# Two transformer blocks on one core: the first feed-forward's down product as seven block products

## The reference

```python
h2 = rms_norm(x, norm2_g[l])
up = h2 @ w_up[l]                      # 1024 x 5632: gate and value
up = causal_depthwise_conv(up, ffn_dw_w[l])   # width 3, along the tokens
gate, val = jnp.split(up, 2, axis=-1)
x = x + (jax.nn.silu(gate) * val) @ w_down[l]  # 2816 -> 1024
```

## Time and profile before

| | |
|---|---|
| median of 3 runs | 2779.06 us |
| profiled execution | 2782.16 us, of which span 2780.5 us |
| granted TensorE clock, mean | 0.992 of 2.4 GHz |
| TensorE busy | 2714.4 us (98%) |
| VectorE, ScalarE, GpSimd busy | 1758.4, 1131.0, 640.6 us |
| DMA | 414 MB, mean 149 GB/s |

### The profile page before, as it was taken

The page is one execution under the profiler, slowest core; times in us unless marked ns, Lnnn a source line. Parts: engine busy times, 40 slices in busy tenths (PEclk is TensorE's granted clock), DMA queues, the critical chain, the costliest instruction groups (busy, mean ns, idle before and its releaser), DMA issues.

```text
span 2780.5 us, 31459 instructions
## 1 busy us (share of the span) xinstructions
PE 2714.4 (98%) x12219; PEld 2197.0 (79%) x12219; DVE 1758.4 (63%) x2235; ACT 1131.0 (41%) x1590; POOL 640.6 (23%) x548
## 2 busy tenths in 40 slices
PE   9989999999999999999999999999999999999997
PEld 7877668788888788888878888766777888888886
DVE  6886554689999843243324444566548787776567
ACT  4423442343433443221235655665345322223543
POOL 1213111000110042010002222113423244444113
PEclk9999999999999999999999999999999999999999
DMA  3224532334444464344623232666543365657874
GB/s 123 84 83 140 145 80 103 140 104 122 130 121 121 157 234 138 117 150 157 214 84 102 69 99 85 173 183 189 195 169 125 137 213 188 204 189 248 262 251 133
DMA packets 147283, 414.45 MB, mean 149 GB/s; under 512 B 18616, under 2 KB 23352, under 8 KB 147136
## 3 DMA queue, kind: packets, MB, share of 16 engines
q1 hardware_dynamic: 115024, 309.97, 34.3%
q0 software_dynamic: 32112, 102.48, 11.9%
HBM read 309.46 MB, written 102.92 MB: 148 GB/s over the span
## 4 chain that ended last, share of the span: by engine, by line
PE 79%; DVE 12%; ACT 4%; issue 3%; DMA 2%; POOL 1%; SPq 0%; DVEq 0%; POOLq 0%; ACTq 0%
PE ps L218 77%; DVE cacc L189 3%; PE ps L221 2%; ACT PB L183 1%; POOL ga L186 1%; DVE cv L189 1%; DVE PB L189 1%; DVE tr L189 1%; DVE tl L186 0%; DVE YA L186 0%; DMA raw<-in_w_win 0%; DVE sqacc L186 0%; DVE ps L198 0%; DVE T L189 0%; DMA RBc<-scr_inv 0%
## 5 line engine op out<-in xcount | busy, mean ns | idle before, releaser
L218 PE MATMUL ps<-AH,wh 128*128 128x512 f32 (+1 forms) x1104 | 446.0, 404 | 19.4 <-DVE T L186 7.0
L218 PE MATMUL ps<-AH,wl 128*128 128x512 f32 (+1 forms) x1104 | 432.0, 391 | 0.0
L218 PE MATMUL ps<-AL,wh 128*128 128x512 f32 (+1 forms) x1104 | 431.6, 391 | 0.0
L218 PEld LDWEIGHTS ps<-AH,wh 128*128 128x128 f32 (+1 forms) x1104 | 206.6, 187 | 72.2 <-issue 10.4
L218 PE MATMUL ps<-stk,stk 128*128 128x512 f32 (+3 forms) x832 | 245.1, 409 | 12.8 <-DVE small L198 6.9
L218 PEld LDWEIGHTS ps<-AH,wl 128*128 128x128 f32 (+1 forms) x1104 | 206.5, 187 | 46.6
L218 PEld LDWEIGHTS ps<-AL,wh 128*128 128x128 f32 (+1 forms) x1104 | 207.0, 187 | 44.4 <-issue 2.9
L218 PEld LDWEIGHTS ps<-stk,stk 128*128 128x128 f32 x832 | 147.9, 191 | 83.2 <-issue 34.0
L186 DVE TENSOR_TENSOR wl<-raw,wh 128x1024 fp32r<-128x1024 f32 (+1 forms) x76 | 112.7, 1484 | 150.2 <-ACT wh L183 135.0
L218 PE MATMUL ps<-euh,ewt 128*128 128x512 f32 x640 | 198.8, 391 | 2.1 <-DVE eul L186 2.1
L186 POOL TENSOR_TENSOR wl<-raw,wh 128x1024 fp32r<-128x1024 f32 (+3 forms) x47 | 102.0, 2171 | 319.3 <-ACT wh L183 319.2
(11 more groups left out here) (324 smaller groups left out, 6373.6 us busy)
## 6 DMA issues: line engine op xcount, KB each, us to landing
ewr<-in_dn SPq DMA_DIRECT2D x88, 256.0 KB, 3.2
pwr<-in_w_up SPq DMA_DIRECT2D x38, 512.0 KB, 4.1
swr<-in_w_gu SPq DMA_DIRECT2D x38, 512.0 KB, 4.1
raw<-in_w_w2in SPq DMA_DIRECT2D x32, 512.0 KB, 4.2
scr_u<-cv SPq DMA_DIRECT2D x22, 512.0 KB, 2.6
eur<-scr_u SPq DMA_DIRECT2D x44, 256.0 KB, 3.4
scr_u<-uu SPq DMA_DIRECT2D x22, 512.0 KB, 8.6
alr<-in_dn POOLq DMA_DIRECT2D x11, 1024.0 KB, 9.9
```

The lines of the kernel that those rows point to most:

```text
L218: return Issued(self, self.e.matmul(out, l, r, start=start, stop=stop, skip_group_check=onto))
```

## The change

FF1's down product uses seven block products with 11 steps each (77 steps, `DOWN1`, `INTO1`), with four sums of weight blocks (`s_s1`) and four of activation blocks (`s_t1`), both kept in DRAM.

1. `weight_sums` in `pool_a`: 88 transfers from DRAM to DRAM of 256 KB in 8 phases of 11 (44 copies, 44 that add), four behind each low part of tiles 4 to 25. From phase 2 on, a phase waits until all before have landed.
2. `block_sums` in `pool_ff1`: GpSimd loads a pair of spilled stages, makes four sums, stores them; 11 times, nine within the up part.
3. Down part: both streams are loaded and split at each step (77 + 77), all low parts on VectorE; passes accumulate onto banks of earlier passes and are evacuated in between.
4. Up part: the seven products go to three banks (bank 0: X11, T2, T3, T4; bank 1: T1, X22; bank 2: X21), double-buffered over pairs; X22 and T3 change places. ScalarE copies bank 0 after X11 and after T2 and bank 1 after T1; `shared` and `shared_end` on VectorE go. `value` (one half) stands before the low parts of the next pair's second group, `gate_end` and `value_scaled` behind, `value_end` is one scaled evacuation.
5. `sums_high` first negates two of the four sums on ScalarE.
6. Value weights are loaded in three transfers with waits of their own, the first two earlier. The first two stage tiles of the down part have other homes (free later), and the last three weight rows use slots 6 to 8.
7. The next stage works in banks 4 to 7 at first, its norm sums in other banks.

```diff
+            for x in range(4 * (s - 4), min(4 * (s - 3), 8 * NK)):   # pool_a, behind w_low(s)
+                if x >= 0:
+                    weight_sums(x)
...
+        def weight_sums(x):
+            phase, k = divmod(x, NK)
+            a11, a21, a12, a22 = [self.io["dn1"][2 * k + i, h, :, :] for i in range(2) for h in range(2)]
+            s2, s3, s4, s1 = [self.io["s_s1"][i, k, :, :] for i in range(4)]
+            if phase > 1:
+                q.wait_ge(S.jd1, 16 * phase * NK)
+            if phase == 0:
+                q.dma(s1, a21).then_inc(S.jd1, 16)
+            elif phase == 1:
+                q.dma(s3, a11).then_inc(S.jd1, 16)
+            elif phase == 2:
+                q.dma_add(s1, a22, max_dma_last_dim=8192).then_inc(S.jd1, 16)
+            elif phase == 3:
+                q.dma_add(s3, a21, max_dma_last_dim=8192).then_inc(S.jd1, 16)
...
+            odd = self.TR1[k][:, 1:4:2, :]          # sums_high
+            q.act(odd, odd, ACT.Copy, scale=-1.0).then_inc(S.th1)
+            q.wait_own()
             q.act(self.TH1[k], self.TR1[k], ACT.Copy).then_inc(S.th1)
...
             for i in range(7):                      # pe_ff1, up part
+                if i == 0:
+                    q.wait_ge(S.uev, 2 * (PLAIN + n - 1) if n else 0)
+                elif i == 2:
+                    q.wait_ge(S.snp1, 3 * n + 1)
+                elif i == 4:
+                    q.wait_ge(S.snp1, 3 * n + 2)
+                elif i == 5:
+                    q.wait_ge(S.snp1, 3 * n + 3)
+                elif i == 6:
+                    q.wait_ge(S.ev1, 3 * n + 2)
                 part(n, i)
-        for w in range(88):
+        for w in range(7 * NK):
...
             taken(n)                                # act_ff1, per pair
             if n:
                 silu(i)
             if n + 1 < NQ:
+                high(n + 1, 0)
+            taken_shared(n)
+            if n + 1 < NQ:
+                high(n + 1, 4)
+            else:
+                d_high(0)
+                u_high(0)
+            taken_fifth(n)
+            if n + 1 < NQ:
+                high(n + 1, 5)
+                high(n + 1, 2)
...
             if n:                                   # dve_ff1, per pair
                 value_end(n - 1)
                 taps(0, i)
+                taps(1, i)
             gate(n)
             if n:
                 gated(i)
             if more:
                 s_sums(n + 1)
+                s_lows(n + 1, 0)
             value(n)
             if more:
+                s_lows(n + 1, 2)
+            gate_end(n)
+            value_scaled(n)
+            if more:
+                s_lows(n + 1, 1, 3)
...
+        def block_sums(j):                          # pool_ff1
+            q.wait_ge(S.tl1, 4)
+            q.wait_ge(S.jd1, self.SUMS1_END + 16 * j)
+            q.wait_ge(S.du1, 32 * j + 32)
+            for x in range(2):
+                q.dma(self.TW1[:, 2 * x:2 * x + 2, :], self.io["s_u1"][2 * j + x, :, :]...).then_inc(S.jl1, 16)
+            ...four q.tt(..., ALU.subtract), each waiting for the one before
+            q.dma(self.io["s_t1"][j, :, :, :], self.TW1[:, :, :]).then_inc(S.jd1, 16)
```

More of the change, by code:

```diff
@@ L381, in __init__ @@
         self.EU, self.EUR, self.EU_FREE = [], [], []
[L382 to L389, removed]
+        homes = [("g", k, 0, 1) for k in range(4)] + [("g", 4, 0, 2), ("g", 5, 0, 2), ("g", 4, 1, 6), ("g", 5, 1, 6)]
+        homes += [("a", k, 1, 7) for k in (0, 1, 2)] + [("a", 6, 1, 7), ("a", 7, 1, 7)]
+        homes += [("a", k, 1, 7) for k in (4, 5, 3)] + [("g", k, 1, 7) for k in range(4)]
         for which, k, half, free in homes:
@@ L395, in __init__ @@
             self.EU_FREE.append(free)
+        for x in range(2):
+            one = Area(nc, sq + 4096 * x, sq + 4096 * x + 4096)
+            self.EUR.append(Area(nc, one.lo + 2048, one.hi).get("eur", [P, 512])[:, :])
+            self.EU.append(tuple(one.get("eu", [P, 512], F32R)[:, :] for _ in range(2)))
+            self.EU_FREE.append(7)
+        self.TW1 = Area(nc, sq, sq + 8192).get("tw1", [P, 4, 512])
         w = Area(nc, lo + 4096, TOP)
@@ L1558, with f1_bank @@
     PAIRS1 = [(part, i) for i in range(PLAIN) for part in ("g", "v")]
-    SHAPE1 = [("X11", 0), ("X21", 1), ("T2", 5), ("T1", 4), ("X22", 6), ("T3", 2), ("T4", 3)]
-    E_FREE = {slot: max(w for w in range(88) if w % DW == slot) for slot in range(DW)}
+    SHAPE1 = [("X11", 0), ("X21", 1), ("T2", 5), ("T1", 4), ("T3", 2), ("X22", 6), ("T4", 3)]
+    def f1_bank(self, n, x):
+        return self.bank(4 * ((n + 1) % 2) + x)
+    DOWN1 = [(("a", 0, 0), ("b", 0, 1)), (("a", 1, 0), ("b", 1, 1)), (("s", 0), ("t", 2)), (("s", 3), ("t", 1)),
+             (("s", 1), ("t", 0)), (("s", 2), ("b", 1, 0)), (("a", 1, 1), ("t", 3))]
+    INTO1 = [((0, 1, ALU.subtract),), ((0, 1, ALU.subtract),), ((0, 0, ALU.subtract),),
+             ((0, 0, ALU.add), (4, 0, ALU.subtract)), ((4, 0, ALU.add),), ((0, 0, ALU.subtract),), ((4, 1, ALU.add),)]
+    SUMS1_END = 16 * 8 * NK
+    SQUARES1 = [(1, n) for n in range(4)] + [(0, n) for n in (4, 5, 6, 7, 0, 1, 2, 3)] + [(1, n) for n in range(4, 8)]
+    E_SLOT = [w % DW for w in range(74)] + [6, 7, 8]
+    E_FREE = {slot: max(w for w in range(77) if w < 74 and w % DW == slot or w == 68 + slot > 73) for slot in range(DW)}
     def f1_tile(self, x):
@@ L1620, in part @@
             name, b = self.SHAPE1[i]
-            out = self.s_bank(n, i)
-            q.wait_ge(S.sl1, 4 * n + {0: 1, 1: 1, 5: 2, 6: 2, 4: 3, 2: 4, 3: 4}[b])
+            out = self.f1_bank(n, (0, 2, 0, 1, 0, 1, 0)[i])
+            first, onto = i in (0, 1, 3), i not in (0, 1, 3)
+            q.wait_ge(S.sl1, 4 * n + {0: 1, 1: 1, 4: 2, 5: 3, 6: 3, 2: 4, 3: 4}[b])
             h, l = self.p_high(n, b), self.p_low(n, b)
@@ L1628, in part @@
                 xh, xl = self.sums1(name, k)
-                q.mm(out, h[:, ws], xh, k == 0, False)
-                q.mm(out, h[:, ws], xl, False, False)
-                t = q.mm(out, l[:, ws], xh, False, k == 3)
+                q.mm(out, h[:, ws], xh, first and k == 0, False, onto)
+                q.mm(out, h[:, ws], xl, False, False, onto)
+                t = q.mm(out, l[:, ws], xh, False, k == 3, onto)
             t.then_inc(S.prd1)
@@ L1742, in act_ff1 @@
         tap_value(1)
-        for b in (0, 5, 4, 2):
+        for b in (0, 4, 5, 2):
             high(0, b)
@@ L1804, in act_ff1 @@
+                q.act(self.sqF[m % 2][:, :], self.XR[:, n, c], ACT.Square).then_inc(self.squared1(m)[0])
+        for w in range(6, 7 * NK):
+            d_high(w)
+            u_high(w)
+            if 52 <= w < 56:
+                square(w - 52)
+            if 63 <= w < 67:
+                square(4 + w - 63)
+                into(0, 4 + w - 63)
+            if 72 <= w < 76:
+                square(8 + w - 72)
+                into(0, w - 72)
         for n in range(4):
@@ L2159, in sp_ff1 @@
         u_load(9)
-        for w in range(9, 88):
+        for w in range(9, 7 * NK):
             d_load(w)
-            if w < 21:
+            if w < 7 * NK - 1:
                 u_load(w + 1)
```

363 lines of the change are left out of this document (194 added, 169 removed), and 4 rows, old and new, of the table SHARED.

## The result

The changed kernel takes 2794.57 us (median of 10 runs, 2784.27 to 2799.72) against 2780.03 for the kernel before (10 runs): ratio 1.0047, 95% interval 1.0035 to 1.0059. It is slower by 14.5 us, and the prediction (2760, faster by 0.7%) was wrong. Its profiled execution has a span of 2796.0 us.

What follows compares the result with a forecast made beforehand. TensorE was taken to bound all of it; -29.9 (down product) -1.2 (its start) +5.0 (up part) +6.0 (weight sums) +0.5 (end) = -19.6 us, from a median of 2779.06 to 2759.5, called 2760; range 2748 to 2774.

Steps and rivals of the forecast that it cites:

- weight sums +6.0: Front, 30 to 290 us: GpSimd's 88 transfers delay low parts that TensorE wants; +6.0 us, bounds 0.5 and 22.
- I take 0.89 and 5.2 for adds, 0.55 and 3.4 for copies: Front: assumed us to issue and to land one 256 KB DRAM-to-DRAM transfer, taken from the nearest trace rows.
- end just as its high part is ready: 0: Front, tile 18: three copies and a wait of 3.4 us end with its high part, so no gap.
- absorbs it: Front, tile 10: 4 us late, but ahead of the 7.04 gap for DVE T, which hides it.
- Rival 2: Slow adds: they land like 1 MB loads, so the front costs +22 and not +6; 2775 us, chance 0.13.
- 0 per pair, with 0.7 as thinnest cover: Up part: tighter waits for banks cost nothing per pair; T2's wait for ScalarE's copy has 0.7 us to spare.
- POOL's block sums are hidden: Up part: GpSimd's 44 additions in 357 us were to cost TensorE nothing.
- Rival 3: Up part: T2 waits in every pair, VectorE slowed beside GpSimd; 2788 us at 1.5 a pair, chance 0.10.
- Pair 0 and the negations: ScalarE's extra negations: +1.15 in plain stages and a 3.4 us T2 gap in pair 0; +5.0 in all.
- X22 in the last pair: TensorE waits 3.1 us for ScalarE's late fifth-bank copy; with clock it replaces 5.9 of old gaps: -1.2.
- The down part: 88 steps become 77, 132 matmuls fewer: -29.9 us, with loads and VectorE keeping up and no new gap.
- The end: Next stage's weight load moves from five steps ahead of the end to three: +0.5 us, bounds 0 and 2.

Runs made afterwards that it cites:

- run 4: Changed kernel with its weight sums and phase waits in place, but the 44 adding transfers made plain copies: 2777.42 us, ratio 0.9995 to the kernel before.
- run 8: Changed kernel without GpSimd's four additions in each block sum, all transfers kept: 2787.20 us, ratio 1.0015 to the kernel before.
- run 6: Changed kernel with GpSimd's last two block sums held until the last pair's sixth product is done: 2793.46 us, ratio 1.0039.
- run 9: Changed kernel with weight sums spread over attention, output product and FF1's start, fifth-bank copy first, last two block sums held: 2769.68 us, ratio 0.9952.
- run 7: Changed kernel without ScalarE's negation of two of the four activation sums, so some products get a wrong sign: 2795.84 us, ratio 1.0043.
- run 11: Run 10's kernel with two activation sums made with opposite sign on VectorE, so ScalarE's negation goes: 2769.46 us, ratio 0.9961.
- run 5: Changed kernel with ScalarE's copy of the fifth bank ahead of the first down step's high parts in the last pair: 2791.17 us, ratio 1.0037.
- run 2: Changed kernel with all 88 weight-sum transfers moved behind the projections, block sums starting one pair later: 2777.59 us, ratio 0.9988.
- run 10: Run 9's kernel with the last two block sums held to the third down step and pair 0's bank copy before the tap: 2768.42 us, ratio 0.9963.

## Why the prediction was wrong

**The step that failed** is the term "weight sums +6.0", above all the durations that it rested on: "I take 0.89 and 5.2 for adds, 0.55 and 3.4 for copies". It measured 26.7 in the front, and its upper bound of 22 was too low as well. The adds land in 7.3 and then 11.0 us (medians), the copies in 4.8 and 6.3; the cost of an issue was right (0.83 for one add). Tile by tile:

- Tile 13: 3.13 for a forecast of 3.0, behind a wait of 4.70 for adds. This place was right in mechanism and size.
- Tile 18, of which the prediction said "end just as its high part is ready: 0", has the 5.52: the wait for copies lasts 6.98 and not 3.4, and the high part is late by its load. The 1.5 at tile 19 did not come, so that the gap which the forecast had near 238 us is another tile's.
- Tile 10 has 6.03, and the wait for DVE T, which "absorbs it", only went from 7.04 to 5.00, so that 4.0 is left. In run 4, with copies, the same wait took up most of it.
- Tile 21, among those that "have room", has 3.74, behind the wait of 10.88 for adds. The 3.1 for the load of q in the attention stood in no term.
- The clock: less the waits of the table under run 4, about 6 us of the 26.7 are left, for which I had counted 1.5. TensorE, with its gaps, was granted 0.91 and 0.92 of the clock over two stretches (0.96 before). By the tables of stretches its busy time per matmul is 80.83/377 = 0.214 against 72.96/353 = 0.207, and 0.218 against 0.207 in the second; times 377 and 337 matmuls that is some 6 us.

Rival 2 had the late landings alone, for +22.

On the size of one transfer, the trace of the kernel before gave 5.2 for an add into SBUF, and no run shows a lone DRAM add; of all 88 the shortest, a copy, landed in 2.7 us, no add in under 4.1, and the longest in 14.9. By the formula of the Trainium skill ("DMA: Bandwidth & Descriptors", Anatomy of one DMA), which I weighed and left, one transfer lands in an estimated 2.6 us: only the quickest copies here do.

**The up part**, "0 per pair, with 0.7 as thinnest cover", held in most pairs: four of them have gaps of 0.2 to 0.5 in this profile (one to seven in those of other runs). "POOL's block sums are hidden" was the failed sentence: run 8 puts 6.7 us on them in the up part and 3.3 in the down part. Rival 3 named the mechanism, and I excused it with a balance of busy times ("5.2 us per two pairs, within the 2 x 2.8 that it gains"; its own working gives 2.6 per pair, and run 8 has 2.2, a busy time of 300.8 for 342.0 over 19 pairs). The size was not the fault: 31 us over 19 pairs is 3.3 per two. The additions themselves took 1.70 on the mean and not 1.29. What decides, as the rows of the last pair read, is which instruction is hit, the low part or the tap ahead of the one evacuation that T2 waits for, and there no balance helps. On this the Trainium skill's rule ("SBUF — State Buffer", Who interferes with whom) and runs 6, 8 and 9 agree: VectorE's work with two SBUF inputs is held up, here 0.69 to 1.75 and 1.22 to 2.27, and the evacuation from PSUM not at all.

**Pair 0 and the negations**: the gap came (2.48 for 3.4) and the plain stages grew by 1.6 for 1.15. Whether the negations cost this is open: run 7 without them is shorter in both places but not in the whole, and run 11 without them has plain stages of 73.3 again and, for T2's gap in pair 0, one of 2.88 ahead of X22.

**X22 in the last pair**: right in mechanism, 3.47 for 3.1, of which about 1 us is contention that the forecast had not (runs 5 and 8).

**The down part**: right as to the matmuls (-29.9) and the pace at 220 GB/s. The gap of 2.33 at its start, not forecast, is contention again (run 8: 0.29). **The end**: 1.49 and some clock for 0.5, as the first load of the next stage lands in 7.1 us and not 4.2 (issued at 1188.88, its high part at 1196.01).

By the ledger the miss of 35 us is 21 in the front, 10 of contention (its up and down shares), and 4 in the end and the rest. Open is how the 15.7 of the adding divides between its own landing, the longer phase waits and the loads that it delays, as no run has one without the other.

## What to carry to other kernels

A transfer between two places in DRAM that adds is not a copy with another opcode: price it by its own measurement, with the loads that run beside it. And a wait for a transfer's landing, for a copy too, does not belong on an engine that also makes what the bound engine waits for: here such waits lasted 4.7 to 10.9 us. Work that is hidden by a balance of busy times is hidden only if no instruction of the thin chain runs beside it; look at which instructions it will meet, not at how many. When such work is moved, ask at once what stands behind it in the new place: here the same cost came back at the gate/value addition (run 2), in the taps (run 9) and in front of a load (run 10), and what won was to spread it over stretches in which nothing that TensorE soon waits for stands behind it.

## What was not expected of the hardware

- 256 KB from DRAM to DRAM: copies land in 3.7 to 6.8 us by stretch (medians), adds in 7.3 in the stretch with some 140 GB/s and in 11.0 in that with 249. Loads of 512 KB on the other queue take 8.9 beside the adds in the last stretch (median of 3), 6.4 with copies in their place; over the front 6.9 (of 8), and 3.5 in the kernel before.
- While GpSimd adds in SBUF (a 128x512 addition takes 1.7 us, 2.0 beside the taps), VectorE's instructions with two SBUF inputs take about 1.0 us longer each, whatever their length: 0.69 becomes 1.75, 1.22 becomes 2.27 (4.54/2), the taps' 1.30 becomes 2.28 (4.56/2). One with an input in PSUM keeps its 0.68.
